# An encoder trunk in one launch: the ConvFFN up-projection without GpSimd

## The reference

```python
def dwconv(x, w, b, left):            # out[t] = sum_k w[k] x[t-left+k] + b
    ...
def conv_ffn(h, w_in, conv_w, conv_b, w_out):
    u = dwconv(h @ w_in, conv_w, conv_b, 1)          # three taps: left, middle, right
    val, gate = jnp.split(u, 2, axis=-1)             # 3072 channels each
    return (jax.nn.gelu(gate, approximate=True) * val) @ w_out
```

## Time and profile before

| | us |
|---|---|
| median of three runs | 808.24 |
| the profiled execution, its span from first to last instruction | 806.8 |
| PE busy | 731.7 (91%) |
| DVE busy | 618.2 (77%) |
| ACT busy | 460.7 (57%) |
| POOL busy | 229.2 (28%) |
| up-projection of layer 0: evacuations of the chunks, first and last start | 255.90, 389.88 |
| up-projection of layer 1: first and last start on ScalarE (L664) | 612.51, 748.8 |

### The profile page before, as it was taken

One profiled execution on the slowest core, in us unless ns is written; L12 is line 12 of the kernel. 1 busy time (PEld: TensorE's weight loads), 2 busy tenths in 40 slices (PEclk: granted clock), 3 DMA queues, 4 the chain that ended last, 5 costly groups with the idle time before them and its releaser, 6 DMA issues.

```text
span 806.8 us, 15207 instructions
## 1 busy us (share of the span) xinstructions
PE 731.7 (91%) x5892; PEld 582.3 (72%) x5892; DVE 618.2 (77%) x830; ACT 460.7 (57%) x682; POOL 229.2 (28%) x157
## 2 busy tenths in 40 slices
PE   5999999999999999898879998793889998898996
PEld 3888888787877888777768876672668887785443
DVE  4888776777849876877777397999999768768752
ACT  3566575757637565555566265758266665655650
POOL 5301010101102534435313044556042334344200
PEclk9999999999999999999999999987999999999999
DMA  9745363636533545454489313403138464454641
GB/s 300 264 131 184 105 209 105 210 105 209 189 127 125 190 156 185 148 186 159 154 303 374 106 54 105 157 1 104 57 101 258 160 204 157 159 189 158 205 152 52
DMA packets 97665, 131.04 MB, mean 162 GB/s; under 512 B 3496, under 2 KB 65728, under 8 KB 97488
## 3 DMA queue, kind: packets, MB, share of 16 engines
q1 hardware_dynamic: 97616, 130.36, 48.6%
HBM read 129.30 MB, written 1.05 MB: 162 GB/s over the span
## 4 chain that ended last, share of the span: by engine, by line
PE 35%; issue 23%; DVE 19%; POOL 12%; ACT 8%; DMA 2%; POOLq 1%; SPq 0%; ACTq 0%; DVEq 0%
PE ps L1424 9%; PE ps L1425 9%; PE ps L1426 9%; POOL work L1329 8%; DVE w_lo L852 4%; POOL cnow L1327 3%; PE ps L1682 2%; PE ps L1683 2%; PE ps L1684 2%; ACT w_hi L511 2%; ACT y_hi L679 2%; DVE mT L900 1%; DVE hT L904 1%; DVE a_lo L880 1%; DMA stage<-in_ffn_w_out 1%
## 5 line engine op out<-in xcount | busy, mean ns | idle before, releaser
L1424 PE MATMUL ps<-a_hi,w_hi 128*128 128x272 f16 (+1 forms) x1280 | 355.9, 278 | 23.6 <-DVE w_lo L852 16.9
L1425 PE MATMUL ps<-a_lo,w_hi 128*128 128x272 f16 (+1 forms) x1280 | 355.6, 278 | 0.0
L1426 PE MATMUL ps<-a_hi,w_lo 128*128 128x272 f16 (+1 forms) x1280 | 355.5, 278 | 0.0
L852 DVE SCALAR_TENSOR_TENSOR w_lo<-stage,w_hi 128x1024 f16<-128x1024 f32 x232 | 289.2, 1278 | 45.6 <-ACT w_hi L511 45.1
L511 ACT ACTIVATE w_hi<-stage 128x1024 f16<-128x1024 f32 x227 | 228.1, 1047 | 22.7 <-PE ps L1426 11.4
L1424 PEld LDWEIGHTS ps<-a_hi,w_hi 128*128 128x128 f16 x1280 | 125.5, 98 | 53.7 <-DVE w_lo L852 20.8
L1426 PEld LDWEIGHTS ps<-a_hi,w_lo 128*128 128x128 f16 x1280 | 125.5, 98 | 20.7
L1425 PEld LDWEIGHTS ps<-a_lo,w_hi 128*128 128x128 f16 x1280 | 125.6, 98 | 20.6
L1424 PE MATMUL ps<-y_hi,w_hi 128*128 128x272 f16 (+1 forms) x384 | 109.5, 285 | 23.2 <-issue 7.1
L1329 POOL TENSOR_TENSOR work<-work 128x544 f32<-128x544 f32 (+1 forms) x24 | 66.7, 2781 | 165.8 <-ACT work L673 165.8
L1425 PE MATMUL ps<-y_lo,w_hi 128*128 128x272 f16 (+1 forms) x384 | 109.4, 285 | 0.0
(11 more groups left out here) (195 smaller groups left out, 925.8 us busy)
## 6 DMA issues: line engine op xcount, KB each, us to landing
stage<-in_ffn_w_in SPq DMA_DIRECT2D x96, 512.0 KB
stage<-in_ffn_w_out SPq DMA_DIRECT2D x24, 1024.0 KB
stage<-in_ret_w_in SPq DMA_DIRECT2D x16, 1024.0 KB
stage<-in_ret_w_out SPq DMA_DIRECT2D x8, 1024.0 KB
stage<-in_lru_w_in SPq DMA_DIRECT2D x8, 1024.0 KB
stage<-in_ret_w_in SPq DMA_DIRECT2D x14, 512.0 KB
stage<-in_lru_w_out SPq DMA_DIRECT2D x8, 512.0 KB
stage<-in_lru_w_a SPq DMA_DIRECT2D x8, 256.0 KB
```

The source lines that it names most:

```text
L852: dve.scalar_tensor_tensor(out=part(w_lo, gw_lo, c, q), in0=flat(stage, c, q), scalar=W_SCALE, in1=part(w_hi, gw_hi, c, q), op0=ALU.mult, ...
L1424: pe.matmul(o, w_h, x_h, start=start, stop=False)
L1425: pe.matmul(o, w_h, x_l, start=False, stop=False)
L1426: return pe.matmul(o, w_l, x_h, start=False, stop=stop)
```

## The change

The parameter tiles `cnow` and GpSimd's part of the up-projection go. The hardware loops of ScalarE and VectorE over the chunks are written out, so that each instruction can name its own column of `cpar` (`tap_col`). The left tap is no longer a multiply-add of VectorE into `u_cv`: ScalarE makes a scaled copy of the four tiles into a new tile `u_left` (1088 elements per partition, within `work`), right behind the middle tap, and VectorE adds it to all four tiles in one instruction, shifted by one token, behind the right taps. The product and the subtraction are VectorE's; the product stands between the third and the fourth quarter of w_lo, the subtraction behind the fourth. TensorE's and SyncE's streams are the same.

```diff
@@ ScalarE, ffn_chunk @@
-                act.wait_ge(cnow_set, n0 + 1)
-                if behind:
+                if n0 >= 2:
                     act.wait_ge(fy_raw, n0 - 1)
                 for n in range(4):
                     last = act.activation(u_cv[b][:, n, t0:T], u_in[b][:, n, t0:T], ACTF.Identity,
-                                          scale=cnow[b][:, cpar_col(1, n):cpar_col(1, n) + 1],
-                                          bias=cnow[b][:, cpar_col(3, n):cpar_col(3, n) + 1])
+                                          scale=tap_col(layer, j, 1, n), bias=tap_col(layer, j, 3, n))
                 last.then_inc(mid_tap, 1)
+                for n in range(4):
+                    last = act.activation(u_left[:, n, t0:T - 1], u_in[b][:, n, t0:T - 1], ACTF.Copy,
+                                          scale=tap_col(layer, j, 0, n))
+                last.then_inc(left_made, 1)
                 prep(c + 2, 2, i)
                 prep(c + 2, 3, i)
                 act.wait_ge(conv_done, n0 + 1)
...
@@ VectorE, ffn_chunk @@
                 dve.wait_ge(mid_tap, n0 + 1)
-                order = (2, 3, 0, 1)
-                for n in order:
-                    dve.scalar_tensor_tensor(
-                        out=u_cv[b][:, n, t0 + 1:T], in0=u_in[b][:, n, t0:T - 1],
-                        scalar=cnow[b][:, cpar_col(0, n):cpar_col(0, n) + 1],
-                        in1=u_cv[b][:, n, t0 + 1:T], op0=ALU.mult, op1=ALU.add).then_inc(left_tap, 1)
-                for m, n in enumerate(order):
-                    dve.wait_ge(left_tap, 4 * n0 + m + 1)
+                for n in range(4):
                     last = dve.scalar_tensor_tensor(
-                        out=u_cv[b][:, n, t0:T - 1], in0=u_in[b][:, n, t0 + 1:T],
-                        scalar=cnow[b][:, cpar_col(2, n):cpar_col(2, n) + 1],
+                        out=u_cv[b][:, n, t0:T - 1], in0=u_in[b][:, n, t0 + 1:T], scalar=tap_col(layer, j, 2, n),
                         in1=u_cv[b][:, n, t0:T - 1], op0=ALU.mult, op1=ALU.add)
-                last.then_inc(conv_done, 1)
+                last.then_inc(right_tap, 1)
+                dve.wait_ge(right_tap, n0 + 1)
+                dve.wait_ge(left_made, n0 + 1)
+                dve.tensor_tensor(u_cv[b][:, :, t0 + 1:T], u_cv[b][:, :, t0 + 1:T], u_left[:, :, t0:T - 1],
+                                  ALU.add).then_inc(conv_done, 1)
                 prep(c + 2, 2, i)
+                dve.wait_ge(gelu_done, n0 + 1)
+                dve.tensor_tensor(u_y[b][:, :, t0:T], u_y[b][:, :, t0:T], u_cv[b][:, 0:2, t0:T],
+                                  ALU.mult).then_inc(fy_raw, 1)
                 prep(c + 2, 3, i)
+                dve.wait_ge(yhi_made, Y_FFN[layer] + j + 1)
+                dve.tensor_tensor(y_lo[:, 2 * j:2 * j + 2, t0:T], u_y[b][:, :, t0:T], y_hi[:, 2 * j:2 * j + 2, t0:T],
+                                  ALU.subtract).then_inc(fylo_made, 1)
...
@@ GpSimd: ffn_chunk, ffn_in and their calls @@
-                pool.tensor_copy(cnow[b][:].unsqueeze(1), cpar[:, layer, one, :]).then_inc(cnow_set, 1)
-                pool.wait_ge(gelu_done, n0 + 1)
-                pool.tensor_tensor(u_y[b][:, :, t0:T], u_y[b][:, :, t0:T], u_cv[b][:, 0:2, t0:T],
-                                   ALU.mult).then_inc(fy_raw, 1)
-                pool.wait_ge(yhi_made, Y_FFN[layer] + b + 2 * i + 1)
...
```

More of the change, by code:

```diff
@@ L167, in build @@
         cpar = sb("cpar", [P, 2, FFN_CHUNKS, 16])
-        cnow = [sb(f"cnow{b}", [P, 16]) for b in range(2)]
         fin_s = sb("fin_s", [P, 8, 2])
@@ L209, in build @@
         u_y = [carve(2, T) for _ in range(2)]
+        u_left = carve(4, T)
         n_parts = KC * CW // 2
@@ L268, in cpar_col, with tap_col @@
             return tap * 4 + n
+        def tap_col(layer, j, tap, n):
+            return cpar[:, layer, j, tap * 4 + n:tap * 4 + n + 1]
         def tiles(v):
@@ L338, in build @@
         ylo_made = sem("ylo_made")
-        cnow_set = sem("cnow_set")
         u_out = sem("u_out")
         mid_tap = sem("mid_tap")
-        left_tap = sem("left_tap")
+        left_made = sem("left_made")
+        right_tap = sem("right_tap")
         conv_done = sem("conv_done")
@@ L651, in _, with ffn_chunk @@
                     estimate_input(1, 0)
-            def ffn_chunk(layer, first_in, i, b):
+            def ffn_chunk(layer, first_in, j):
                 t0 = ffn_first(layer)
+                i, b = divmod(j, 2)
                 c = first_in + b
-                n0 = layer * FFN_CHUNKS + b + 2 * i
-                behind = layer > 0 or not (isinstance(i, int) and i == 0)
+                n0 = layer * FFN_CHUNKS + j
                 act.wait_ge(u_out, n0 + 1)
-                act.wait_ge(cnow_set, n0 + 1)
-                if behind:
+                if n0 >= 2:
                     act.wait_ge(fy_raw, n0 - 1)
@@ L676, in ffn_chunk @@
                 act.wait_ge(fy_raw, n0 + 1)
-                dst = y_hi[:, bass.ds(4 * i + 2 * b, 2), t0:T] if not isinstance(i, int) else \
-                    y_hi[:, 4 * i + 2 * b:4 * i + 2 * b + 2, t0:T]
-                act.activation(dst, u_y[b][:, :, t0:T], ACTF.Copy).then_inc(yhi_made, 1)
+                act.activation(y_hi[:, 2 * j:2 * j + 2, t0:T], u_y[b][:, :, t0:T], ACTF.Copy).then_inc(yhi_made, 1)
                 prep(c + 3, 1, i)
@@ L684, in ffn_in @@
                 prep(first_in + 2, 1)
-                for b in range(2):
-                    ffn_chunk(layer, first_in, 0, b)
-                with act.Fori(1, FFN_CHUNKS // 2) as i:
-                    for b in range(2):
-                        ffn_chunk(layer, first_in, i, b)
+                for j in range(FFN_CHUNKS):
+                    ffn_chunk(layer, first_in, j)
             ffn_in(0, FFN0_IN)
@@ L1317, in sum_input @@
                 sum_tiles(sum_h, DT, t0, h_sq, i * DT)
-            def ffn_chunk(layer, i, b):
-                t0 = ffn_first(layer)
-                n0 = layer * FFN_CHUNKS + b + 2 * i
-                dynamic = not isinstance(i, int)
-                if layer or dynamic:
-                    pool.wait_ge(conv_done, n0 - 1)
-                one = bass.ds(2 * i + b, 1) if dynamic else slice(2 * i + b, 2 * i + b + 1)
-                pool.tensor_copy(cnow[b][:].unsqueeze(1), cpar[:, layer, one, :]).then_inc(cnow_set, 1)
-                pool.wait_ge(gelu_done, n0 + 1)
-                pool.tensor_tensor(u_y[b][:, :, t0:T], u_y[b][:, :, t0:T], u_cv[b][:, 0:2, t0:T],
-                                   ALU.mult).then_inc(fy_raw, 1)
-                pool.wait_ge(yhi_made, Y_FFN[layer] + b + 2 * i + 1)
-                two = bass.ds(4 * i + 2 * b, 2) if dynamic else slice(4 * i + 2 * b, 4 * i + 2 * b + 2)
-                pool.tensor_tensor(y_lo[:, two, t0:T], u_y[b][:, :, t0:T], y_hi[:, two, t0:T],
-                                   ALU.subtract).then_inc(fylo_made, 1)
-            def ffn_in(layer):
-                for b in range(2):
-                    ffn_chunk(layer, 0, b)
-                with pool.Fori(1, FFN_CHUNKS // 2) as i:
-                    for b in range(2):
-                        ffn_chunk(layer, i, b)
             pool.memset(v_hi[:, 2, :], 0.0).then_inc(zeroed, 1)
@@ L1364, in _ @@
             sum_input(1, 0)
-            pool.wait_ge(par_ready, 1)
-            ffn_in(0)
             sum_output(1, 0)
@@ L1416, in _ @@
             sum_input(3, T0_LRU_OUT)
-            ffn_in(1)
         @block.tensor
```

8 lines of the change are left out of this document (3 added, 5 removed).

## The result

The changed kernel takes 779.93 us (median of 4 runs, 779.34 to 780.76) against 808.27 us (807.37 to 809.7, 4 runs) before: a ratio of 0.9649, 95% interval 0.9635 to 0.9663. Its profiled execution took 780.1 us with a span of 778.3 us.

What follows compares the result with a forecast made beforehand. The prediction took a ring through GpSimd's order, 12.44 us a chunk against TensorE's 11.13, to bound the up-projections. Savings of 14.2, 2.2 and 12.1 us gave 806.8 - 28.5 = 778.3 for the span, 779.7 as median; range 776.7 to 783, chance 0.82.

Steps and rivals of the forecast that it cites:

- The ring: Up-projection: a closed loop of waits through GpSimd, ScalarE and VectorE takes 12.44 us a chunk; TensorE wants 11.13 in layer 0.
- The walk: Up-projection chunk after the change, timed step by step from the evacuation: next evacuation at 10.13 us, 9.85 in layer 1.
- the sum: Whole kernel: layer 0 stalls 14.2, half clock 2.2, layer 1 stalls 12.1 us; together 28.5 us off the span.
- The eight pieces: Up-projection chunk: copy, middle, left and right taps, gelu, product, y_hi, subtraction; 12.05 us plus handovers of about 0.05 each.
- the upper end: VectorE's new addition: at most L1159's 2.3 us, measured beside a working GpSimd; 1.29 was taken.
- half clock: TensorE behind the 4.6 us gate-weight stall of layer 0: clock 0.52 in the mean over 4.6 us; removing it saves 2.2.
- The gate weights: Layer 0, fourth down-projection chunk: needed 33.4 us after the last evacuation; y_hi at 8.5 instead of 15.0, so the stall goes.
- the allowance of 3 us for the clock elsewhere: TensorE's clock from 520 to 545 us, mean 0.86: slow stretches may shift as that stage moves; 3 us either side.
- VectorE as the bound: Rival, up-projection: VectorE's ring grows to 11.2 to 11.4 us in layer 0; 783 to 788 us, chance 0.08.
- the lead: TensorE starts each up-projection with two chunks of weights in hand, lasting until 326.39 in layer 0, 668.10 in layer 1.
- The gate stall stays: Rival, layer 0 down-projection: transfers hold the stage-slot chain, so 7.0 us come back; 786.7 us, chance 0.04.
- VectorE's fixed order: Rival, up-projection: product ahead of quarter 3's residue waits for gelu and starves TensorE; 818 us, chance of slower 0.02.

Runs made afterwards that it cites:

- the run with the middle taps on ScalarE: Changed kernel, with the recurrent layer's middle taps moved from GpSimd to ScalarE activations; 777.22 us.
- the next one: Changed kernel with recurrent middle taps on ScalarE, and also the four operations 0.5*a + 0.5 moved from GpSimd to ScalarE; 774.06 us.
- four additions: Changed kernel with four more VectorE additions of 544 columns in every up-projection chunk, into tiles nothing reads; 811.04 us.
- two additions: Changed kernel with two more VectorE additions of 544 columns in every up-projection chunk, into tiles nothing reads; 781.17 us.

## Why the prediction was right

**The ring.** It was read as closed through GpSimd's order, and either opening alone, the copy's or the product's, gives all of the gain, while the loops give next to nothing. The walk gave VectorE 10.13 us in layer 0 and 9.85 in layer 1; 10.00 and 9.75 (606.24 to 615.99) were measured. It gave waits of 1.0 and 0.7 us for TensorE; they are 1.03 and 0.72. The walk did not see that one opening is enough: the sum was made for the whole change, and beside one opening the rest of it is spare. One piece of the reading was wrong without harm: the product's 2.71 us were put down to GpSimd. By its end, 1.4 of them are a wait for VectorE's two conversions, which start at 350.10 and have ended at 352.36, and 1.3 come behind. The eight pieces still added up, as gelu and product cover the same stretch, and the forecast took the whole stretch away. Where only a part of it went, in the run with the left tap alone, the same reading missed by 8.5 us.

**The prices.** Addition 1.29 expected and 1.29 measured, product and subtraction 0.72 and 0.72, left taps 1.7 and, for four, 1.74 us or 1.64 from start to start. (The 597 ns set against 519 mix two widths; at 272 columns the middle taps' mean is 602.) L1159's 2.3 us, the upper end, was GpSimd's doing: the same operation takes 2.32 us in the run with the middle taps on ScalarE, beside a GpSimd product that ends 1.15 us before it, and 1.28 in the next one, where no GpSimd product has started before it.

**The sum.** Stalls and half clock of layer 0: 16.4 expected, 16.5 measured; layer 1: 12.1 and 12.3. The gate weights: last y_hi 8.4 us after the last evacuation (373.82 to 382.22), 8.5 expected; the conversion to w_lo of the fourth down-projection chunk starts 26.5 us after it (400.28) and its first quarter is done 1.2 us later, needed at 33.4; no stall and no half clock there. That the total came out on 778.3 to the tenth is partly luck: -1.3 us ahead of the up-projection and +1.7 in the recurrent layer were not in the sum and nearly cancel. The first is 0.6 at the first load and about 0.7 in slow matmuls at the start: 17 of them before and 10 after are 0.23 us apart instead of 0.116, half the pace, though the profile's clock reads 1.00 there in both. The second is mostly a stretch in which nothing of the change happens; after (columns as in the earlier trace rows):

```profile
564.00:568.00 4.00, 3.80 (x21) 2.83 (x22) 3.54 (x4) 2.44 (x4) 0.00 (x0) 0.61 0.34 98
```

Before, the same matmuls (582 to 586) had 1.00. This is the allowance of 3 us for the clock elsewhere. It need not go with the change: with the parameters in place alone, where TensorE stalls as little as in the changed kernel, the layer takes 128.58 us and the span is 776.0; with four additions, which stalls like the kernel before, it takes 128.58 as well; with the product alone 130.20, with two additions 130.23. Why the clock falls there in some executions and not in others was not settled.

**The rivals.** VectorE as the bound: refuted as a description of this kernel, and true in layer 0 from a ring of about 11.6 us on: with 11.27 the lead pays, with 12.53 the cost is 31 us. The gate stall stays: no; it came back when the ring was made long (5.07 us and the half clock). VectorE's fixed order: nothing near it; the one wait of 1.3 us for a gelu is that for its table load in the first chunk.

The 11.6 is an estimate: eleven rings may exceed TensorE's 11.12 us by the lead together. The expectations took 6.0 us for it; from the changed kernel's rows it comes to about 5.3 us, 0.5 for each ring: the last quarter of w_lo for the third chunk is done at 265.44, and TensorE, which starts on that chunk at about 262.4 (329.12 less six chunks of 11.12), comes to it 8.35 us later. No run has a ring between 11.27 and 12.53.

## What to carry to other kernels

Follow a stall round until you are back where you began: if the way passes twice through one in-order engine, the instruction that joins the two is worth the whole difference of the rings, whatever its own price, and moving either side opens it. Cost the ring against the bound engine's period and against the lead that it starts with: here two more operations a chunk cost 1.2 us in all, and the next two 29.9. Before giving GpSimd something beside a busy VectorE, count what VectorE's neighbouring operations become. And look at where a long GpSimd operation ends, not only at how long it is: if it always ends the same time after a VectorE operation, the ring goes through VectorE.
